# q and k turned and split in the projection and loaded as score operands by attention; three panel tile banks

## The reference

```python
xn = _rmsnorm(x, norm1_w)
q, k, v, f_raw, z, xbc, dt_raw, g_att, g_ssm = _split_proj(xn @ w_in)
q = _rmsnorm(q.reshape(b, T, N_HEADS_ATT, HEAD_DIM), q_norm_w)
k = _rmsnorm(k.reshape(b, T, N_HEADS_ATT, HEAD_DIM), k_norm_w)
logf = jax.nn.log_sigmoid(f_raw + b_f)
# _fox_attend, c = cumsum(logf); for the stream, cached k, v, logf stand ahead
s = jnp.einsum('bqhd,bkhd->bhqk', q, k) * ATT_SCALE
s = jnp.where(kpos[None, :] <= qpos[:, None], s + (cq - ck), -jnp.inf)
att = jnp.einsum('bhqk,bkhd->bqhd', jax.nn.softmax(s, axis=-1), v)
# then: causal convolution and SSD on xbc, gates, two branch projections merged, w_out, MLP
```

## Time and profile before

| | us |
|---|---|
| median of three runs | 2888.79 |
| lowest, highest | 2885.17, 2889.52 |
| the profiled execution | 2885.89 |
| its span, first to last instruction | 2884.1 |
| mean granted TensorE clock in it | 0.978 of full speed |

### The profile page before, as it was taken

One profiled execution on the slowest core, in us unless ns is written; L12 is line 12 of the kernel. 1 busy time (PEld: TensorE's weight loads), 2 busy tenths in 40 slices (PEclk: granted clock), 3 DMA queues, 4 the chain that ended last, 5 costly groups with the idle time before them and its releaser, 6 DMA issues. The chain is left out here.

```text
span 2884.1 us, 47789 instructions
## 1 busy us (share of the span) xinstructions
PE 2737.1 (95%) x18754; PEld 2658.0 (92%) x18754; DVE 1577.2 (55%) x2867; ACT 1022.4 (35%) x2353; POOL 405.7 (14%) x475
## 2 busy tenths in 40 slices
PE   6998979999999999997999989998989999999999
PEld 5997978989999889887999979998989999999999
DVE  4336337656566565565898864464373444434434
ACT  4223336556666655653434331121231111111110
POOL 0000012212122222222555520000000000000000
PEclk8999999999999999998999999999989999999999
DMA  3222232132232222215888873343221111111112
GB/s 115 90 90 53 79 90 91 43 101 76 67 108 76 66 93 58 84 63 140 205 194 214 201 203 121 112 134 128 65 99 58 45 44 45 44 45 44 48 67 96
DMA packets 334448, 273.31 MB, mean 95 GB/s; under 512 B 95952, under 2 KB 311632, under 8 KB 334096
## 3 DMA queue, kind: packets, MB, share of 16 engines
q1 hardware_dynamic: 334224, 270.25, 32.9%
HBM read 197.90 MB, written 72.28 MB: 94 GB/s over the span
## 5 line engine op out<-in xcount | busy, mean ns | idle before, releaser
L411 PE MATMUL banks<-w_hi,xn_hi 128*128 128x256 f32 x1440 | 407.8, 287 | 8.7 <-DVEq L368 5.0
L411 PE MATMUL banks<-w_lo,xn_hi 128*128 128x256 f32 x1440 | 405.5, 286 | 0.0
L414 PE MATMUL banks<-xn_hi,w_hi 128*128 128x352 f32 x1152 | 379.5, 329 | 0.7 <-ACT att_xs L986 0.7
L414 PE MATMUL banks<-xn_hi,w_lo 128*128 128x352 f32 x1152 | 378.7, 329 | 0.0
L414 PE MATMUL banks<-xn_lo,w_hi 128*128 128x352 f32 x1152 | 378.2, 328 | 0.0
L411 PE MATMUL banks<-w_hi,xn_lo 128*128 128x256 f32 x1280 | 366.3, 286 | 0.0
L411 PEld LDWEIGHTS banks<-w_hi,xn_hi 128*128 128x128 f32 x1440 | 276.7, 192 | 10.6 <-DVEq L368 5.1
L411 PEld LDWEIGHTS banks<-w_lo,xn_hi 128*128 128x128 f32 x1440 | 276.6, 192 | 0.2
L1704 PE MATMUL banks<-h_hi,w_hi 128*128 128x352 f32 x768 | 248.8, 324 | 1.9 <-DVEq L1625 1.9
L1704 PE MATMUL banks<-h_lo,w_hi 128*128 128x352 f32 x768 | 248.6, 324 | 0.0
L1704 PE MATMUL banks<-mlp_uhi,w_hi 128*128 128x352 f32 x768 | 248.6, 324 | 0.0
(11 more groups left out here) (293 smaller groups left out, 6160.8 us busy)
## 6 DMA issues: line engine op xcount, KB each, us to landing
w_raw<-in_w_in SPq DMA_DIRECT2D x44, 1024.0 KB, 5.5
scratch_xbc<-att_co SPq DMA_DIRECT2D x32, 512.0 KB, 2.6
ssd_ab<-scratch_acum SPq DMA_DIRECT2D x64, 256.0 KB, 6.0
br_g<-scratch_gates SPq DMA_DIRECT2D x72, 176.0 KB, 2.8
scratch_gates<-hand_tanh SPq DMA_DIRECT2D x48, 176.0 KB, 5.4
scratch_z<-att_z_stage SPq DMA_DIRECT2D x64, 128.0 KB, 1.9
ssd_xbc<-scratch_xbc SPq DMA_DIRECT2D x64, 128.0 KB, 3.4
ssd_xbc<-scratch_xbc SPq DMA_DIRECT2D x128, 64.0 KB, 3.7
```

What stands on the lines that cost most here:

```text
L411: ins = self.nc.tensor.matmul(self.bank(n, P, PW), x[:, k, t * P:(t + 1) * P], w[:, k, :], start=first, stop=end)
L414: ins = self.nc.tensor.matmul(self.bank(n, P, TT), w[:, k, m * P:(m + 1) * P], x[:, k, r * TT:(r + 1) * TT], start=first, stop=end)
```

## The change

q and k are turned and split once, in the projection, and stored in DRAM as ready score operands: `q_ops` and `k_ops`, per head 64 rows of one part, 64 of the other, and the four bias rows. 44 groups (`groups`): four of cached k in slots 0 to 3 of the first round, then five per q or k panel, one per slot from the fourth slot after the panel's last tile. A group is four transposes of 128 columns (two small ones for the stream's tokens) into bank 4 (the decays' use of that bank moves to 3), a hi copy on ACT with the scale and q's norm weight in it, a subtraction on DVE, and four stores of 64 rows (eight, where the group goes to two places). The sum of squares is now made tile by tile. q is no longer stored by rows, nor multiplied by its weight on DVE. In attention `prep`, `make_hi`, `make_lo` and `double` are gone; `load_ops` loads both operands of a score with their bias rows, k's first one twice; the loads of KS move one unit later, and the panel tiles rotate over banks 4, 6 and 7.

```diff
 class HeadNormTm:
...
+    def groups(self, i, n):
+        out = []
+        if i == 0 and 0 <= n < self.CACHED:
+            out.append((n, None))
+        for g in range(self.GROUPS):
+            for k in self.ended(n - 4 - g):
+                out.append((self.CACHED + (i * self.per + k) * self.GROUPS + g, (k, g)))
+        return out
...
     def start_sp(self, sp):
...
+        sp.dma_start(rows.rearrange("p (t n) -> p t n", t=2), self.cache_k.rearrange("(t p) n -> p t n", p=P)).then_inc(self.cached, 16)
...
     def act(self, act, i, n):
...
             s.nc.scalar.activation(self.stage[x][0:m, t, :], s.bank(n, m, PW), ACT.Copy).then_inc(self.copied, 1)
-            s.nc.scalar.activation(self.sq[0:m, t, :], s.bank(n, m, PW), ACT.Square).then_inc(s.free, 1)
+            if u:
+                act.wait_ge(self.summed, u)
+            s.nc.scalar.activation(self.sq[0:m, :], s.bank(n, m, PW), ACT.Square).then_inc(s.free, 1)
+        for c, src in self.groups(i, n - 1):
+            w = self.width(src)
+            act.wait_ge(self.turned, c + 1)
+            if c >= 2:
+                act.wait_ge(self.ops_stored[c % 2], self.landed(c - 2))
+            s.nc.scalar.activation(self.t_hi[c % 2][:, 0:w], s.core.banks[:, self.B_TURNED, 0:w], ACT.Copy,
+                                   scale=self.scale(src)).then_inc(self.hi_made, 1)
...
     def dve(self, dve, i, n):
...
-            v.tensor_reduce(self.ss[:], self.sq[:].rearrange("p t (h d) -> p (t h) d", d=HD), AX.X, ALU.add).then_inc(self.meaned, 1)
...
+        for k, t in s.mine(self, n):
...
+            s.wait_free(dve, i, n)
+            v.tensor_reduce(self.ss[k % 2][0:m, t * self.HEADS:(t + 1) * self.HEADS], self.sq[0:m, :].rearrange("p (h d) -> p h d", d=HD),
+                            AX.X, ALU.add).then_inc(self.summed, 1)
+        for c, src in self.groups(i, n - 1):
+            w = self.width(src)
+            dve.wait_ge(self.hi_made, c + 1)
+            bank, hi, lo = s.core.banks[:, self.B_TURNED, 0:w], self.t_hi[c % 2][:, 0:w].bitcast(F32), self.t_lo[c % 2][:, 0:w]
+            v.scalar_tensor_tensor(out=lo, in0=bank, scalar=self.scale(src), in1=hi, op0=ALU.mult, op1=ALU.subtract).then_inc(self.lo_made, 1)
...
+    def pe(self, pe, i, n):
+        s = self.stream
+        for c, src in self.groups(i, n):
+            if src is None:
+                pe.wait_ge(self.cached, 16)
+            elif src[1] == 0:
+                self.wait_normed(pe, i, src[0])
+            if c:
+                pe.wait_ge(self.lo_made, c)
+            for rows, m, col in self.blocks(c, src):
+                ins = s.nc.tensor.transpose(s.core.banks[:, self.B_TURNED, col:col + m], rows, s.core.ident[0:m, 0:m])
+            ins.then_inc(self.turned, 1)
...
     def sp(self, sp, i, n):
...
+        for c, src in self.groups(i, n - 1):
+            sp.wait_ge(self.lo_made, c + 1)
+            for head, x, cols, col in self.places(i, c, src):
+                at = (HD, 0) if x == 0 else (0, HD)
+                w = cols.stop - cols.start
+                for part, buf in zip(at, (self.t_hi, self.t_lo)):
+                    for b in range(2):
+                        sp.dma_start(self.ops[x][head + b, part:part + HD, cols],
+                                     buf[c % 2][b * HD:(b + 1) * HD, col:col + w].bitcast(F32)).then_inc(self.ops_stored[c % 2], 16)
...
                 for n in range(stream.slots):
                     stream.pe(pe, i, n)
+                    norm.pe(pe, i, n)
                     if last:
                         decays.pe(pe, n)
...
-    B_SCORES, B_TURNED, B_PREP, B_OUT, B_TILES = 0, 2, 4, 5, (6, 7)
+    B_SCORES, B_TURNED, B_OUT, B_TILES = 0, 2, 5, (4, 6, 7)
...
+            def load_ops(h, g):
...
+                if g == QA or g == QB:
...
+                    sp.dma_start(first, q_ops[h, 0:2 * HD, cols]).then_inc(ops_loaded[g], 16)
+                    sp.dma_start(second[0:KX, :], q_ops[h, HD:HD + KX, cols]).then_inc(ops_loaded[g], 16)
                 else:
...
+                    for b in range(2):
+                        sp.dma_start(first[b * HD:(b + 1) * HD, :], k_ops[h, 0:HD, cols]).then_inc(loaded, 16)
+                    sp.dma_start(second[0:KX, :], k_ops[h, HD:HD + KX, cols]).then_inc(loaded, 16)
...
             stream.start_sp(sp)
-            load(0)
-            for g in SEQ:
-                load_bias(0, g)
+            load_ops(0, K0)
+            load_ops(0, QA)
+            load_v(0)
+            for g in (K1, QB, KS):
+                load_ops(0, g)
...
+                    for g in {0: (K0,), 1: (QA,), 3: (K1, QB), LASTU: (KS,)}.get(u, ()):
+                        load_ops(h + 1, g)
...
             stream.pe(pe, 0, 0)
+            stream.pe(pe, 0, 1)
             pe.wait_ge(padded, 2)
-            prep(0, K0)
-            prep(0, QA)
-            stream.pe(pe, 0, 1)
             scores(0, 0)
...
+            stream.pe(pe, 0, 2)
             scores(0, 1)
```

More of the change, by code:

```diff
@@ L464 @@
     HEADS = PW // HD
[L466 to L473 removed]
+    GROUPS = 5
@@ new lines, with __init__ @@
+    CACHED = 4
+    B_TURNED = 4
+    def __init__(self, sb, sem, per, weights, k_to, q_ops, k_ops, cache_k):
+        self.per, self.weights, self.to, self.ops, self.cache_k = per, weights, k_to, (q_ops, k_ops), cache_k
+        self.stage = [sb(f"norm_stage{x}", [P, NT + 1, PW]) for x in range(2)]
+        self.sq, self.ss = sb("sq", [P, PW]), [sb(f"ss{x}", [P, (NT + 1) * self.HEADS]) for x in range(2)]
+        self.w, self.w_q = sb("norm_wk", [P, HD]), sb("norm_wq", [P, 1])
+        self.t_hi, self.t_lo = ([sb(f"turned_{n}{j}", [P, 512], F32R) for j in range(2)] for n in ("hi", "lo"))
+        self.w_loaded, self.cleared, self.copied, self.cached = sem("w_loaded"), sem("cleared"), sem("copied"), sem("cache_loaded")
+        self.summed, self.meaned, self.rooted, self.scaled = sem("summed"), sem("meaned"), sem("rooted"), sem("scaled")
+        self.inverted, self.weighted = sem("inverted"), sem("weighted")
+        self.stored, self.turned, self.hi_made, self.lo_made = sem("norm_stored"), sem("turned"), sem("turned_hi"), sem("turned_lo")
+        self.ops_stored = [sem(f"ops_stored{j}") for j in range(2)]
@@ new lines, in blocks @@
+    def blocks(self, c, src):
+        if src is None:
+            rows = self.stage[1][:].rearrange("p t n -> p (t n)")
+            return [(rows[:, t * D + (2 * c + b) * P:t * D + (2 * c + b + 1) * P], P, (2 * b + t) * P) for b in range(2) for t in range(2)]
+        k, g = src
+        stage = self.stage[k % 2]
+        if g == 4:
+            return [(stage[0:TS, NT, b * P:(b + 1) * P], TS, b * TS) for b in range(2)]
+        return [(stage[:, 4 * (g % 2) + t, g // 2 * P:(g // 2 + 1) * P], P, t * P) for t in range(4)]
@@ new lines, in places, with width @@
+    def places(self, i, c, src):
+        if src is None:
+            return [(4 * c + 2 * b, 1, slice(TP, TP + PAST), b * PAST) for b in range(2)]
+        k, g = src
+        head = (i * (self.per // 2) + k // 2) * self.HEADS
+        first = 0 if k % 2 == 0 else PAST
+        if g == 4:
+            return [(head + 2 * b, k % 2, slice(TP + first, TP + first + TS), b * TS) for b in range(2)]
+        return [(head + g // 2 * 2, k % 2, slice(g % 2 * 512, (g % 2 + 1) * 512), 0)]
+    def width(self, src):
+        return 2 * TS if src is not None and src[1] == 4 else 512
@@ new lines, in wait_normed @@
+    def wait_normed(self, eng, i, k):
+        if k % 2:
+            eng.wait_ge(self.weighted, (i * self.per + k) // 2 + 1)
+        else:
+            eng.wait_ge(self.scaled, i * self.per + k + 1)
+    def start_sp(self, sp):
+        sp.dma_start(self.w[:], self.weights[1].to_broadcast([P, HD])).then_inc(self.w_loaded, 16)
+        with self.stream.nc.allow_non_contiguous_dma(reason="one value per partition"):
+            for b in range(2):
+                sp.dma_start(self.w_q[b * HD:(b + 1) * HD, :], self.weights[0].rearrange("o (d e) -> d (o e)", e=1)).then_inc(self.w_loaded, 16)
+        rows = self.stage[1][:].rearrange("p t n -> p (t n)")[:, 0:2 * D]
+        sp.dma_start(rows.rearrange("p (t n) -> p t n", t=2), self.cache_k.rearrange("(t p) n -> p t n", p=P)).then_inc(self.cached, 16)
@@ L538, in finish @@
     def finish(self, sp):
-        for x in range(2):
-            sp.wait_ge(self.stored[x], 32 * (self.stream.rounds * (self.per // 2) + 1))
+        count = self.CACHED + self.stream.rounds * self.per * self.GROUPS
+        sp.wait_ge(self.stored, 32 * (self.stream.rounds * self.per // 2))
+        for j in range(2):
+            sp.wait_ge(self.ops_stored[j], self.landed(count - 1 - (count - 1 - j) % 2))
 class Decays:
@@ L2038, in _ @@
                     turn(h, u, g)
-                for g in prepared(h, u, 1):
-                    prep(h + 1, g)
                 stream_parts(h, u, 1)
@@ L2045, in _ @@
                     product(x, h, u, g)
-                for g in prepared(h, u, 2):
-                    prep(h + 1, g)
```

(4 more changed lines are left out.)

286 lines of the change are left out of this document (87 added, 199 removed).

## The result

| | before | after |
|---|---|---|
| median, us (runs) | 2889.13 (4) | 2934.57 (4) |
| lowest, highest | 2885.17, 2889.52 | 2929.25, 2937.85 |
| the profiled execution, its span | 2885.89, 2884.1 | 2937.85, 2936.1 |
| mean granted clock in it | 0.978 | 0.967 |

The ratio is 1.0159, with a 95% interval of 1.0139 to 1.0178: the change costs 45 us. Predicted were 33, at 2922, in a range of 2880 to 2958. A repetition beside the later experiments gave 1.0163 (1.0149 to 1.0177).

A forecast was written before the change was run, and what follows sets the result against it. PE, busy 95% of the span, was taken to bound the kernel. Projection +62 us, clock +14 and attention -43 gave +33 on the median of 2888.8, so 2922 us, in a range of 2880 to 2958.

The forecast's parts named there:

- The added wait: Projection: PE waits for DVE's subtraction 19 times, 2.1 us lost each; twelve in three undisturbed q panels cost 25 us.
- D: Rival: turned buffers stored late in v panels (10 us), w_raw 4.4 late three times (13); 2945 us, chance 0.12.
- The decay chain: Projection, fourth q panel: group 0's subtraction stands behind DVE's scans; 12 us longer, 10 without transposes, one wait near 12.
- The transposes: 44 groups turned on PE in the projection, 36 at 0.44 and 8 at 0.2: 17 us.
- The clock: Projection: idle stretches of PE make its clock fall to half, ten falls at 1.4 us: 14 us, range 0 to 32.
- The start: Start of the projection: cached groups' waits 6.3 us, later first split on ACT about 2; together 8 us.
- The end of the stage: End of the projection: eight small stores of the last group issued ahead of v's, 1.5 us.
- Attention: Attention shorter by 43 us: 34 of transposes leaving PE, 6 at the stage's start, 3 of small waits.
- rival A: The prediction itself, with PE's waits at the z starts staying in attention; +33 us, 2922 us, chance 0.50.
- C: Rival: waits at the eight z starts in attention vanish too and the clock holds; -17 us, 2872 us, chance 0.16.
- The third bank: Attention: a third tile bank lets PE run one tile further ahead of ACT's copies, worth 0 to 1 us.
- even: Attention: w_raw up to 4.4 us later three times, against five fewer loads ahead of it; -6 to +13 us.

The follow-up runs named there:

- early: After, with the hi copy on ACT and the subtraction on DVE ahead of the slot's own tile work in the projection; 2892.66 us, 1.0034 of before.
- act_only: After, with only ACT's hi copy moved ahead of the tile's work and DVE's order left; one run, 2934.24 us.
- best: After with early's order, subtraction also ahead of DVE's fold, first w_raw ahead of cached k, K1 and QB later for ten heads; 2879.64 us, 0.9968 of before.
- two: After with two tile banks in attention in place of three; 2936.13 us, 1.0168 of before.
- late: After with K1 and QB of the next head loaded one unit later, together with KS, in attention; 2942.67 us, 1.0200 of before.
- best2: After with early's order, raw7's w_raw place, K1 and QB later for ten heads, 68-row loads as 64 and 4, old start; 2865.68 us, 0.9925 of before.
- raw7: The kernel early with the w_raw load issued two slots later in the projection; 2877.85 us, 0.9967 of before.
- fill: After with 17 unread matmuls on PE ahead of each of the 11 long waits of the projection's first round; 2924.21 us, 1.0134 of before.

## Why the prediction was right, and where it was off

**The added wait: right in place and cause, nearly in size.** Forecast were waits of PE at the turning line for DVE's subtraction, some 19 of 1.95 idle (2.1 lost), none beside v tiles. There are 18 of 2.05 to 2.17 (2.3 lost), where they were put: one of the decay panel's four has another length, 7.34. The twelve forecast at 25 us cost 28. Two short ones came beside v tiles, 0.73 and 1.04 us, of which more under D. The working gave 344.35 - 342.25 = 2.1; the chain read from the earlier trace rows is the chain in the trace. Two terms were a little short: q's hi copy with its weight takes 0.69, not 0.59, and its subtraction 0.75 for 0.685. Early shows the cause, act_only that both queues carry it.

**The decay chain: right in sum by luck, wrong in form.** +12 was forecast without the clock, 1.9 of them transposes; compared matmul by matmul the stretch is 11.9 longer, but PE worked 14.3 us more of it at the low level than before. By the 44% of above this is 6.2 us of clock, so some 5.7 are left where 12 were forecast, and some 4 for the chain's 10. In the repetition, with less low clock and a longer wait, the stretch is 9.4 longer. The subtraction of group 0 does stand behind the scans (start, duration):

```profile
305.14 3.80 DVE L738 TENSOR_TENSOR_SCAN qkv_dec_u<-qkv_ones,qkv_dec_e 32x128 f32<-32x128 f32 x9
...
309.91 0.74 DVE L603 SCALAR_TENSOR_TENSOR qkv_turned_lo<-banks,qkv_norm_wq,qkv_turned_hi 128x512 fp32r<-128x512 f32 x1
...
310.71 1.11 PE L628 MATMUL banks<-ident,qkv_norm_stage 128*128 128x128 f32 x4 [7.34 <-DVE qkv_turned_lo L603]
```

But there is no wait near 12 us left at the chain's end: PE's 10.7 has become 3.24 for the scaled panel, 7.34 here, and three of 2.11, and when these are over the chain is done. In early the same stretch is 4.6 longer than in before.

**The transposes: right.** A block moves its successor by 0.42 to 0.44 in the projection. For those taken out of attention see there.

**The clock: the term that was mis-sized, in the number of falls.** Ten falls at 1.4 were taken, 14 us. The low stretches grew by 58 us, as much as 17 of 3.4 us, and at 1.5 each these are 25 us; behind the 60 us summed without the clock, the projection's 85.4 leave 25 too. So the price was nearly right, and the number was not: in after 16 of the 18 waits had a stretch behind them, in the repetition 13. The two falls of three in the earlier trace rows would have given 12 to 13, and no reason was given for ten. That the 60 us fit is partly luck: the chain's 10 were 6 too many, while the twelve waits were 3 and the two beside v tiles 2 short. From span to span 19 us lie between forecast and measurement (52 and 33); 11 are the clock, 3.4 the end of the stage, 4 the noise of the rest.

**The start: right.** Cached groups and start were 6.3 and 2. Compared matmul by matmul the first slots are 12.7 longer: 1.8 of transposes, 3.0 of clock, and 7.9.

**The end of the stage: too small.** Eight stores were taken at 1.5 us, and they are 5.0 of SP, of which 4.9 show. The row that told this was there: the earlier trace rows has an issue at 0.60.

**Attention: right in sum, -42.5 for -43, its terms less so.** Forecast were 34 of PE's work and 9 of its waits; by the windows (the earlier trace rows without the gap of 10 us, and above) PE is busy 38 us less and idle 4.6 less. What the 38 are beside the 320 transposes was not looked into. The idle at the z starts stayed, as rival A had it against C: eight panels, 24 us before and 27 now. What they wait for was taken too simply, though. It was put to DVE's inverse behind the convolution; at the first and third z panel it was w_raw behind the operand loads, as rival D had it, and best shows that 11 us could be had there. The third bank was taken at 0 to 1, and two shows no more.

**D was right in its mechanisms and small in its sum.** The loads of 68 rows keep 4.2 packets in flight, and w_raw landed 8.3, 8.7 and 9.6 us after its issue at the first three z panels where it takes 5.4, 5.7 and 6.8 in late: 3 us late where 4.4 were taken. Attention still came out at the forecast; that the five fewer loads elsewhere made up for it, as the prediction's "even" has it, is not shown, since no run takes them apart. The ring of two showed too, beside the v tiles, where D put it: ACT's hi copy of k's fourth group waits 2.24 and 2.55 us for the stores of the group two before in the first round, and PE behind it (the second time):

```profile
242.13 0.60 ACT L571 ACTIVATE qkv_turned_hi<-banks 128x512 fp32r<-128x512 f32 x1 [2.55 <-DMA scratch_k_ops<-qkv_turned_lo]
...
243.51 0.31 PE L628 MATMUL banks<-ident,qkv_norm_stage 32*128 32x32 f32 x2 [1.04 <-DVE qkv_turned_lo L603]
```

That is 2 us where D had 10; in early, with PE no longer late, the ring decided what was left.

What stays open: what is left at the z starts of best2, and how many of the 5 us between the stages another order on SP would save; neither was tried. A ring of three buffers in place of raw7's order was not run. Why one idle stretch of 2 to 2.6 us is followed by the low clock and the next is not stays open.

## What to carry to other kernels

When an edit puts a step between two stages of a pipeline, write down for each engine what stands ahead of that step in its queue in the same slot: here a copy and a subtraction of 0.7 us each, which could have run on idle engines, cost some 40 us because both were listed after work that wasn't ready yet, and moving the copy alone opened nothing. Charge a wait of PE with what the clock takes behind it as well, 1.5 us for most of them here. When a wait is taken away, look for the buffer ring and the DMA order that it had covered, and give each load the place that its own panel needs and not one rule for all.

## What the runs showed of the hardware

- Idle stretches of 2.1 us on PE, in a kernel that is otherwise busy, were followed by 3.4 us at 1.2 GHz eleven times of twelve in after, and 9, 9, 9 and 8 times of twelve in four more profiles of the same code. At 1.86 us (act_only) it was nine of twelve, and with matmuls put into the stretch none of those filled (fill). In early two of 2.56 and 2.44 us had no low stretch behind them.
- The 3.4 us at 1.2 GHz cost 1.5 us, less than the 1.7 of a halved speed: the matmuls of 256 columns are 0.21 us apart in them and 0.12 outside, and the distance of two groups grows from 5.64 to 7.14.
- A load of 68 rows keeps 4.1 to 4.2 packets in flight, loads of 64 or 128 rows 10 to 16 in their fullest half microsecond; the 196 rows of QB's two operands take 4.5 us, or 2.5 with the 68 split into 64 and 4.
- Stores of 128 KB land in 2.4 us in the median in after. Behind a load of 1 MB issued 0.6 us before the first of them, ACT got their buffer some 6 us after the last had been issued (101.13 against 95.0).
- A store of 64 rows costs SP 0.62 us to issue when several follow each other, whether its rows have 2 KB or 128 bytes: eight small ones are 5 us at the end of a stage.
